# Scores one step ahead, and layer-norm statistics as dense products, in the attention of a two-block float32 kernel

## The reference, cut to what matters

```
hn = rmsnorm(h, norm1_g)                      # 528 positions x 1024
q, k, v, u = split(hn @ w_in)                 # 4 heads, two components of 64 each; v: 128 per head
q, k = rope(q), rope(k)
for each 128-query block, each head:
    s = q_c @ k_c.T / 8 for c = 0, 1;  s = where(key <= query, s, -inf)
    a = softmax(s_0) - lam * softmax(s_1)     # differential attention
    o = a @ v
o = rmsnorm(o, sub_g) * (1 - lam_init)
z = silu(layer_norm(depthwise_conv(glu(u))))  # layer norm over 512 channels
h = h + concat(o, z) @ w_out
```

## Time and profile before

| | us |
|---|---|
| median of 3 runs | 3041.46 (3029.35 to 3041.84) |
| the profiled execution | 3043.26 |
| its span | 3041.4 |
| TensorE busy | 2724.2 (90%) |
| VectorE busy | 1079.2 (35%) |
| ScalarE busy | 973.7 (32%) |
| GpSimd busy | 1204.2 (40%) |
| second layer's attention, 940.9 to 1064.5 | 123.60, of which TensorE 98.00, granted clock 0.77 |

### The profile page before, as it was taken

How to read it: one execution, slowest core, us unless ns; L and a number is a source line. 1 busy time by engine, 2 the same in 40 slices (tenths; PEclk the granted TensorE clock), 3 DMA queues, 4 the chain that set the end, 5 groups by cost and what they waited for, 6 DMA issues and landing times.

```text
span 3041.4 us, 47778 instructions
## 1 busy us (share of the span) xinstructions
PE 2724.2 (90%) x19190; PEld 2439.9 (80%) x19190; DVE 1079.2 (35%) x1795; ACT 973.7 (32%) x1813; POOL 1204.2 (40%) x511
## 2 busy tenths in 40 slices
PE   4987899999798879999959989889999989699999
PEld 4985899999796679999958778778877777587777
DVE  3853422022295332212127754211466622220210
ACT  2333322222333422222234612242456552221221
POOL 3461345545556044555533411032211145454453
PEclk7987999999898789999959989989999989799999
DMA  3220112222221012232212300041111133222221
GB/s 118 70 70 1 56 58 84 94 94 64 79 70 56 1 56 78 74 97 92 75 42 70 97 2 2 1 136 45 60 42 43 42 135 97 69 83 83 84 96 69
DMA packets 174520, 204.13 MB, mean 67 GB/s; under 512 B 6443, under 2 KB 158982, under 8 KB 174102
## 3 DMA queue, kind: packets, MB, share of 16 engines
q1 hardware_dynamic: 170192, 200.05, 20.3%
q10 hardware_dynamic: 4166, 1.84, 0.2%
HBM read 193.48 MB, written 8.39 MB: 66 GB/s over the span
## 4 chain that ended last, share of the span: by engine, by line
PE 77%; issue 7%; POOL 5%; DVE 5%; ACT 3%; DMA 1%; DVEq 1%; ACTq 1%; POOLq 1%; SPq 0%
PE ps L711 16%; PE ps L712 16%; PE ps L713 16%; PE ps L1541 6%; POOL wlo L2684 3%; PE ps L1431 2%; PE ps L809 2%; PE ps L895 1%; PE ps L1413 1%; PE ps L898 1%; PE ps L950 1%; POOL hn_lo L2699 1%; PE ps L912 1%; PE ps L1193 1%; PE ps L1083 1%
## 5 line engine op out<-in xcount | busy, mean ns | idle before, releaser
L2684 POOL TENSOR_TENSOR wlo<-wraw,whi 128x2048 fp32r<-128x2048 f32 x182 | 836.9, 4598 | 1282.8 <-ACT whi L1608 1243.4
L711 PE MATMUL ps<-hn_hi,whi 128*128 128x264 f32 (+1 forms) x2752 | 895.1, 325 | 55.9 <-POOL hn_lo L2699 32.3
L712 PE MATMUL ps<-hn_lo,whi 128*128 128x264 f32 (+1 forms) x2752 | 882.3, 321 | 0.0
L713 PE MATMUL ps<-hn_hi,wlo 128*128 128x264 f32 (+1 forms) x2752 | 880.6, 320 | 0.0
L711 PEld LDWEIGHTS ps<-hn_hi,whi 128*128 128x128 f32 x2752 | 525.9, 191 | 94.5 <-issue 48.8
L1608 ACT CAST whi<-wraw 128x2048 fp32r<-128x2048 f32 x182 | 346.5, 1904 | 667.1 <-PE ps L713 489.1
L713 PEld LDWEIGHTS ps<-hn_hi,wlo 128*128 128x128 f32 x2752 | 524.6, 191 | 36.7
L712 PEld LDWEIGHTS ps<-hn_lo,whi 128*128 128x128 f32 x2752 | 525.9, 191 | 32.6
L711 PE MATMUL ps<-ff_hi,whi 128*128 128x264 f32 x704 | 200.6, 285 | 9.6 <-POOL ff_lo L2774 9.6
L713 PE MATMUL ps<-ff_hi,wlo 128*128 128x264 f32 x704 | 200.4, 285 | 0.0
L712 PE MATMUL ps<-ff_lo,whi 128*128 128x264 f32 x704 | 200.0, 284 | 0.0
(11 more groups left out here) (440 smaller groups left out, 4362.1 us busy)
## 6 DMA issues: line engine op xcount, KB each, us to landing
wraw<-in_w_in SPq DMA_DIRECT2D x54, 1024.0 KB, 5.3
wraw<-in_w_gate_up SPq DMA_DIRECT2D x44, 1024.0 KB, 5.1
wraw<-in_w_up SPq DMA_DIRECT2D x16, 1024.0 KB, 5.5
wraw<-in_w_down SPq DMA_DIRECT2D x16, 1024.0 KB, 4.8
wraw<-in_w_out SPq DMA_DIRECT2D x12, 1024.0 KB, 5.1
wraw<-in_w_down SPq DMA_DIRECT2D x16, 768.0 KB, 4.5
wraw<-in_w_down SPq DMA_DIRECT2D x16, 640.0 KB, 4.3
gate_dram<-gate_out SPq DMA_DIRECT2D x16, 256.0 KB, 2.2
```

The lines of the kernel that those rows point to most:

```text
L711: nc.tensor.matmul(dst, whi[:, slot, c:c + P], rhs_hi, start=start, stop=False)
L712: nc.tensor.matmul(dst, whi[:, slot, c:c + P], rhs_lo, start=False, stop=False)
L713: return nc.tensor.matmul(dst, wlo[:, slot, c:c + P], rhs_hi, start=False, stop=stop)
L2684: nc.gpsimd.tensor_tensor(wlo[:, slot, :], wraw[:, slot, :], whi[:, slot, :].bitcast(F32), ALU.subtract).then_inc(w_split, 1)
```

## The change

It has these parts, all inside the attention of block 1:

1. The first exponential is written to `probs4` in SBUF, as the second was, and the difference reads it there. `scores(u)` waits for `exp_done` of u-2 instead of `diff_ready` of u-2.
2. TensorE issues the scores of u+2 ahead of the transposes of u.
3. `scores(0)` goes ahead of `rotated(3)`.
4. Channel sums become products with a broadcast column of ones as the stationary operand and the chunks as the moving one. They give the 128x528 row image at once, and ScalarE scales or takes the root while it copies. The spreading products, the 128x5 steps and their waits go. The reciprocal is now on 128x528.
5. The square sums stay in iteration 6; root, reciprocal and the four multiplications, Silus and casts are spread over iterations 6 to 10.
6. In the tail's scores the products are grouped by kind: four heads' wide products in a row, then the four narrow ones, then the four masks.
7. The output fills start one iteration later, and those after the loop are placed anew.

```diff
-                def conv_sums():
+                def conv_mean_rows():
                     pe.wait_ge(conv_done, l * 3 + 3)
                     pe.wait_ge(taps_added, l * GROUPS1 + GROUPS1)
-                    for t in range(NT1):
-                        for c in range(4):
-                            last = nc.tensor.matmul(ps[:, 6, t:t + 1], conv[:, c * T1 + P * t:c * T1 + P * t + P],
-                                                    ones[:, 0:1], start=(t == 0 and c == 0), stop=(c == 3),
-                                                    skip_group_check=True)
-                    last.then_inc(ln_sum, 1)
-                def conv_mean_rows():
-                    pe.wait_ge(ln_mean, l + 1)
-                    spread(rms, 20, ln_rows_at).then_inc(ln_mean_rows, 1)
-                def conv_square_sums():
+                    for c in range(4):
+                        for a, w in ((0, 512), (512, LAST)):
+                            last = nc.tensor.matmul(ln_rows_at[:, a:a + w], ones[:, 0:1].to_broadcast([P, P]),
+                                                    conv[:, c * T1 + a:c * T1 + a + w], start=(c == 0), stop=(c == 3),
+                                                    skip_group_check=True)
+                    last.then_inc(ln_mean_rows, 1)
+                def conv_square_rows():
                     pe.wait_ge(ln_sq, l + 1)
                     pe.wait_ge(rope_done, l * KD + KD)
-                    for i in range(NT1):
-                        last = nc.tensor.matmul(ps[:, 6, i:i + 1], sq[:, 0, P * i:P * i + P], ones[:, 0:1],
-                                                start=True, stop=True)
+                    for a, w in ((0, 512), (512, LAST)):
+                        last = nc.tensor.matmul(ln_rows_at[:, a:a + w], ones[:, 0:1].to_broadcast([P, P]),
+                                                sq[:, 0, a:a + w], start=True, stop=True)
                     last.then_inc(ln_stat, 1)
-                def conv_rstd_rows():
-                    pe.wait_ge(ln_rstd, l + 1)
-                    spread(rstd, 20, ln_rows_at).then_inc(ln_rows, 1)
...
                     if u >= 2:
-                        pe.wait_ge(diff_ready, l * UNITS1 + (u - 1))
+                        pe.wait_ge(exp_done, l * UNITS1 + (u - 1))
...
+                scores(0)
                 rotated(3)
-                conv_sums()
-                scores(0)
                 scores(1)
-                extras = {0: conv_mean_rows, 6: conv_square_sums, 7: conv_rstd_rows}
+                conv_mean_rows()
                 f = 0
                 for u in range(UNITS1):
-                    differences_turned(u)
                     if u + 2 < UNITS1:
                         scores(u + 2)
-                    if u in extras:
-                        extras[u]()
-                    elif 1 <= u <= 4:
+                    differences_turned(u)
+                    if 1 <= u <= 4:
                         rotated(u + 3)
-                    elif u >= 10:
+                    elif u == 6:
+                        conv_square_rows()
+                    elif u >= 11:
                         out_fill(f)
                         f += 1
                     values(u)
...
-                            p = probs4[:, u % 2, 1, 0:P * (t + 1)] if c else s[:, 0, :]
                             at = NT1 * hd + t
-                            last = nc.scalar.activation(p, s[:, c, :], ACT.Exp, bias=top, accum_out=mass[:, c, at:at + 1])
+                            last = nc.scalar.activation(probs4[:, u % 2, c, 0:P * (t + 1)], s[:, c, :], ACT.Exp, bias=top,
+                                                        accum_out=mass[:, c, at:at + 1])
...
-                        nc.scalar.copy(mean_sb, ln_rows_at).then_inc(ln_mean_copied, 1)
+                        nc.scalar.activation(mean_sb, ln_rows_at, ACT.Copy, scale=1.0 / 512).then_inc(ln_mean_copied, 1)
...
+                        nc.scalar.activation(mean_sb, ln_rows_at, ACT.Sqrt, bias=eps5, scale=1.0 / 512).then_inc(ln_rms, 1)
-                    if u == 7:
+                    if u == 8:
                         for c in range(4):
...
-                                                   scores_of(u)[:, 0, :], ALU.mult, ALU.add).then_inc(diff_ready, 1)
+                                                   probs4[:, slot, 0, 0:keys], ALU.mult, ALU.add).then_inc(diff_ready, 1)
...
-                    if u == 6:
+                    if u == 7:
                         dve.wait_ge(ln_rms, l + 1)
-                        nc.vector.reciprocal(rstd[:, 20:20 + NT1], rms[:, 20:20 + NT1]).then_inc(ln_rstd, 1)
-                    if u == 7:
-                        dve.wait_ge(ln_rows, l + 1)
-                        for c in range(4):
+                        nc.vector.reciprocal(ln_rows_at, mean_sb)
+                        dve.drain()
+                    if u in (7, 8):
+                        for c in range(2 * (u - 7), 2 * (u - 6)):
                             x = conv[:, c * T1:(c + 1) * T1]
                             nc.vector.tensor_tensor(x, x, ln_rows_at, ALU.mult).then_inc(ln_t, 1)
```

More of the change, by code:

```diff
@@ L876, in scores, with rows_of @@
                         pe.wait_ge(ln_t, l * 4 + 4)
+                        def rows_of(h1):
+                            return slice(32 * h1, 32 * h1 + 32)
                         for c in range(2):
                             for h1 in range(HEADS1):
-                                own = slice(32 * h1, 32 * h1 + 32)
-                                q = q_tail[:, c, h1, :]
-                                nc.tensor.matmul(ps[own, c, :], q, raw(4 + h1, 0, 512), start=True, stop=True)
-                                at = ps[own, 6, LAST * c:LAST * (c + 1)]
-                                nc.tensor.matmul(at, q, raw(4 + h1, 512, LAST), start=True, stop=False,
-                                                 skip_group_check=True)
-                                last = nc.tensor.matmul(at, ident[:, 0:32], causal[:, 0:LAST], start=False, stop=True,
-                                                        skip_group_check=True)
+                                nc.tensor.matmul(ps[rows_of(h1), c, :], q_tail[:, c, h1, :], raw(4 + h1, 0, 512),
+                                                 start=True, stop=True)
+                            for h1 in range(HEADS1):
+                                nc.tensor.matmul(ps[rows_of(h1), 6, LAST * c:LAST * (c + 1)], q_tail[:, c, h1, :],
+                                                 raw(4 + h1, 512, LAST), start=True, stop=False, skip_group_check=True)
+                            for h1 in range(HEADS1):
+                                last = nc.tensor.matmul(ps[rows_of(h1), 6, LAST * c:LAST * (c + 1)], ident[:, 0:32],
+                                                        causal[:, 0:LAST], start=False, stop=True, skip_group_check=True)
                         last.then_inc(scored, 1)
@@ L2300, in _ @@
                                                ).then_inc(sub_mass, 1)
-                for f in range(6, 12):
+                for f in range(5, 10):
                     out_add(f)
```

30 lines of the change are left out of this document (12 added, 18 removed).

## The result

The changed kernel takes 2990.85 us (median of 4 runs, 2988.68 to 2995.29) against 3041.65 us for the kernel before in the same session (4 runs, 3029.35 to 3044.57). The ratio is 0.9842, with a 95% interval from 0.9813 to 0.9872. The forecast was 2985 us with a range of 2964 to 3018. The profiled execution took 2988.68 us, its span is 2986.8 us, and the mean granted clock rose from 0.921 to 0.933.

What follows compares the result with a forecast made beforehand. TensorE, busy for 90% of the span, was taken as the bound. Per layer 3.7 + 10.1 + 17.0 + 0 + 0.9 = 31.7 us saved, 3.5 back for the clock: 28, 56 for both, giving 2985 us (range 2964 to 3018).

Steps and rivals of the forecast that it cites:

- 3.5 for the clock: Per layer, 3.5 us given back because the clock stays low for a while behind two waits of 3 and 5 us.
- T0 to T5: First transposes of unit 0 to those of unit 5, the rotation units: 23.7 us plus 2.0 instead of 35.8.
- T5 to V10: Transposes of unit 5 to values of unit 10: 27.3 us instead of 44.25, 17.0 saved.
- The slot was never the bound: Rival: VectorE's serial rope, maxima and difference bound the loop; only parts 3, 4, 6 count, 3023 us; chance 0.09.
- The rival of a half clock outside the fills: Clock stays at 1.2 GHz outside the fills: 15 us more per layer, 3015 us; chance 0.14.
- the slower outcome: Rival: reordered TensorE stream never earns full clock from 193 to 316 us, 20 us more per layer, 3082; chance 0.04.
- the lock: Two-SBUF-input differences wait for GpSimd in the rotation loop: 2.0 us counted; as full rival +8 per layer, 3001, chance 0.08.
- The Silu wait: Unit 9's transposes to its values: 5.2 us, since ScalarE's table loads and four Silus go ahead of its copy.
- From V10 to V16: Values of unit 10 to values of unit 16, 29.3 us: TensorE has hardly a gap, so nothing saved.
- From there on: Values of unit 16 to fill 16, 25.67 us: one fill more, but it covers two head-row stalls of 2.4; 0.9 saved.
- the fills alone: Argument against the slower outcome: in the kernel before, the output fills alone brought a clock of 1.00.
- signs of being wrong: Clock under 0.7 in the units, maxima still waiting for scores, or differences of 1.5 us beside GpSimd.

Runs made afterwards that it cites:

- experiment 1: Changed kernel with each unit's transposes again ahead of the scores of the unit two later, voiding parts 1 and 2: 3036.27 us, stretches 335.4 us.
- experiment 2: Changed kernel with the score slot free only at the difference again (part 1 alone undone, new order kept): 3018.49 us, stretches 330.9 us.
- experiment 6: Kernel before with only the layer-norm mean sums replaced by eight dense products: 3042.70 us, ratio 1.0020, stretches 351.1 us.
- experiment 9: Changed kernel with the old layer-norm mean: one-column sums, ScalarE's copy and spread products: 2990.92 us, stretches 293.6 us.
- experiment 7: Changed kernel with ScalarE's block of four Silus one unit later, unit 9 instead of 8: 2978.58 us, stretches 296.8 us.
- Experiment 4: Changed kernel with the ratio of the masses computed from one SBUF tensor and two scalars: 2974.09 us, repeated 2970.80; stretches 282.7 and 283.7 us.
- experiment 10: Kernel before with parts 1, 2 and 6 alone (free slot, scores first, grouped tail scores): 2998.52 us, stretches 306.6 us.
- 5: Kernel before with parts 1 and 2 alone: 2998.74 us, ratio 0.9865, stretches 316.2 us.

## Why the prediction was right, and where it was not

It was right in its time (5.9 us off) and in its main mechanism. Step by step, for the first and the second layer, from the marks shown above and the same marks of the second layer. All marks count from the end of the projections.

Added up, the terms give 30.9 and 24.4 us saved in the two layers, where the forecast had 31.7 less 3.5 for the clock, 28.2 in each. The 55.4 us of this profile against the forecast 56 are partly luck: the second profile of the same kernel saved 50.5, since both its layers are like the second one here.

*Parts 1 and 2, the loop.* T0 to T5 was forecast at 25.7 us instead of 35.8 and took 25.2 and 27.0. T5 to V10 was forecast at 27.3 instead of 44.25 and took 27.15 and 27.2. That the scores leave the loop, and that this carries the gain, is shown from both sides: 31.8 us when added alone, 40 when undone, of 53 in all (348.0 to the mean of 295.1). "The slot was never the bound" forecast 9.2 us per layer from the other parts; experiment 1 gives 6.3, and the free slot's 36 us of experiment 2 (28 by the medians) rule the rival out. The rival of a half clock outside the fills is ruled out by 0.91 and 0.89 in the units, and with it the slower outcome. What no step of mine said is that the two parts only pay together.

*Part 3 was mis-sized.* Forecast 3.7 us saved up to the first transposes; 2.15 and 0.6 were. My step had VectorE and ScalarE "done by 200.0, hidden behind it". The ratio was not: it waited for GpSimd until 201.68, and TensorE stood for 0.98 us at the first transposes. Another 0.48 us went ahead of `scores(0)`, which now stands right behind the projections and waits for ScalarE's last copy of them. The sum also began at 193.3, where the kernel before had its rotation already behind it, and counted the rotation again. In the second layer the old sums took 4.5 us, not 6.07, since the clock fell later, so there was less to save. I had priced the lock at one place, the differences beside the squares, and a 4.5 us operation of GpSimd lies beside the first ratio.

*Parts 4 and 5.* Eight dense products took 4.40 us at full clock (4.1 forecast), and the clock between 195 and 200 us is 1.00, not 0.60, as forecast. The reciprocal is one row, forecast 3.5 us:

```profile
234.23 3.46 DVE L2275 RECIPROCAL ps<-mean_sb 128x528 f32<-128x528 f32 x1 [1.55 <-ACT mean_sb L1731]
```

But the gain that I booked for the mean rows is not there: experiments 6 and 9 find nothing in either kernel beyond the spread of the measure. In experiment 6 a duration saved at TensorE, and a clock raised for 10 us, came back as waits and a lower clock further on. The root and the square rows weren't tried by themselves.

*Part 6* was forecast at 4.5 us with bounds of 2.5 and 8, and took 3.54 and 3.8, most of it at half clock; at full clock, in experiment 7, it took 2.1. I had taken the rate of two row strips; four column strips overlap fully. The Trainium skill's factor of 2.38 for three strips ("TensorE: Matmul & The Clock Gate", section "Measured speedup vs the span model"), which I cited, pointed in this direction; the runs show four at the price of one.

*The Silu wait.* From the transposes to the values of unit 9 I forecast 5.2 us, and 5.26 it took, 4.81 of them TensorE's longest wait. In the profile of experiment 7 another place of the Silus saves none of it; the medians leave that open.

*Part 7 and the end.* From V10 to V16 I forecast nothing saved, and 1.2 were. From there on I forecast 0.9 saved, by a mark that was the last quarter of fill 16 and not its start. With the last fill as the mark it is none in the first layer (52.8 before, 52.9 after), and in the second 3.2 us are lost. There the granted clock is 0.66 behind the one-column head sums. The same sums stand at the same place in the first layer, where it is 1.00 (285 to 290 us above), so they do not decide it alone. The fill's products between two groups of sums run 0.22 us apart instead of 0.12, with TensorE busy throughout:

```profile
1007.00:1012.00 5.00, 5.00 (x31) 5.00 (x32) 0.43 (x1) 2.21 (x3) 0.00 (x0) 0.66 0.00 0
```

*The clock* was forecast as an allowance of 3.5 us per layer that goes back, and a stage up to V16 "with a clock over 0.9". That stage took 91.0 and 92.8 us, as forecast (92), at 0.89 and 0.87. In the units (to about 75 us behind the projections) the clock is 0.91 and 0.89. My sentence that before "the fills alone" had brought 1.00 was wrong by the earlier trace rows, units at full clock. The half clock in both stretches fell from 126 us to 58 (68 in the second profile). That short waits bring the full clock was counted; that each wait put back or taken away moves the clock as well, by as much as the wait's own size or more in experiments 2 and 4, was not.

*The lock* was forecast at 2.0 us per layer for the differences, with bounds of 0 and 10. Two of them lengthened, from 0.48 to 1.63 us and from 0.75 to 1.48, which is 1.9: the term was right. One of my signs of being wrong, differences of 1.5 us beside GpSimd, did show, though at the forecast price. Not counted was the first ratio, 2.8 us longer than alone. Experiment 4 removes a part of all this, and 6 us per layer go, of which 1.3 to 2.1 are the instructions and the rest goes with the clock. So the term was right for the instructions and too low for what they set off.

The remaining 11.5 us between experiment 10 and the changed kernel (306.6 to 295.1) belong to parts 3, 4, 5 and 7 together: the mean rows, for which experiment 9 finds nothing, the square rows, the order of the first rotation, the spreading of the Silus and casts, and the fills. They were not told apart.

## What to carry to other kernels

When a slot and the order in front of it hold the same work back, change both: the free slot alone brings nothing, the order alone brought 4.5 us of the stretches (18 by the medians), both brought 32 to 40. A duration taken from TensorE in front of a loop that waits is not a gain until the wait behind it is looked at, and a gain of a few us in a loop with idle TensorE can double, or vanish, through the granted clock. Read such edits over the stretch that they touch and by the median of the whole, and trust what both show: here the rest of the program moved by 22 us between profiles, and not evidently by chance alone. Beside a long GpSimd operation look at the form of VectorE's small instructions first.

## What the runs showed of the hardware

- Four fp32 products of 32 stationary columns and 512 moving columns, in four different column strips one behind the other, took the time of one: 0.88 us at full clock, 1.71 at half.
- An instruction of one element per partition with two SBUF tensors stood for 3.06 us beside GpSimd's 4.51 us operation and ended with it; with one SBUF tensor and scalar operands it took 0.27 beside the same one.
- The granted clock can fall while TensorE has no idle time: to 0.66 behind the one-column head sums of the second layer (1007 to 1012 us). The same sums ran at 1.00 in the first layer (285 to 290 us).
- In the eight layers with one-column mean sums (before, 5, 9, 10) the half clock began 3.4 to 8.7 us behind the projections, in the twenty with dense mean rows not before 10.4 us.
- The same code outside the two stretches took 2677.5 to 2699.9 us from one profile to the next, with 285 to 362 us of it at half clock. The two do not go strictly together (2677.5 us with 285, 2690.5 with 310, 2678.5 with 319), so the clock as the only cause is not shown.
